# Gated linear attention with two heads below each other in the partitions: 64x64 tiles, no zero padding, output products between the outer products, and head sums ahead of the layer norm

## The reference

```python
b = jnp.cumsum(log_a, axis=2)
q_t = qc * jnp.exp(b); k_t = kc * jnp.exp(-b); k_s = kc * jnp.exp(b_last[:, :, None] - b)
att = jnp.einsum('bnihd,bnjhd->bnhij', q_t, k_t)        # inside a chunk
att = jnp.where(causal, att, 0.0)
o_intra = jnp.einsum('bnhij,bnjhe->bnihe', att, vc)
def step(state, xs):
    o_i = jnp.einsum('bihd,bhde->bihe', q_i, state)     # query times the state before the chunk
    new_state = dec[..., None] * state + jnp.einsum('bjhd,bjhe->bhde', k_i, v_i)
```

```python
v = _layernorm(jax.nn.gelu(v), ln_g, ln_b)     # first branch
q = _rmsnorm(q, q_g); k = _rmsnorm(k, k_g)     # second branch, per head
```

## Time and profile before

| | before |
|---|---|
| median of 3 runs | 1688.66 us |
| the profiled execution | 1690.31 us, its span 1688.5 us |
| PE busy | 1618.3 us (96%) |
| DVE, ACT busy | 1005.9 us (60%), 729.7 us (43%) |
| first transpose of the recurrence to the first gate matmul, layers 0 and 1 | 264.17 to 287.02 us, 783.46 to 808.02 us |
| PE waiting in group `u` and at the start of `za` | 0.55 and 1.70 us in layer 0, 0.56 and 1.74 us in layer 1 |

### The profile page before, as it was taken

One profiled execution on the slowest core, in us unless ns is written; L12 is line 12 of the kernel. 1 busy time (PEld: TensorE's weight loads), 2 busy tenths in 40 slices (PEclk: granted clock), 3 DMA queues, 4 the chain that ended last, 5 costly groups with the idle time before them and its releaser, 6 DMA issues.

```text
span 1688.5 us, 21496 instructions
## 1 busy us (share of the span) xinstructions
PE 1618.3 (96%) x8009; PEld 1326.6 (79%) x8009; DVE 1005.9 (60%) x2246; ACT 729.7 (43%) x1503; POOL 57.8 (3%) x80
## 2 busy tenths in 40 slices
PE   6999999999999999999999999999989999998999
PEld 6878777788887878777788887999767789985667
DVE  4597656444444397757443344486876554788663
ACT  4444443333234443543332434434456553354662
POOL 0000002000001000002000001000000010000000
PEclk9999999999999999999999999999999999999999
DMA  6332121323323223112233323332112233211121
GB/s 219 93 92 71 42 63 51 100 88 100 100 94 96 85 87 88 51 50 63 76 96 92 99 90 110 104 88 60 57 38 69 76 95 92 83 56 38 38 76 62
DMA packets 80883, 136.23 MB, mean 81 GB/s; under 512 B 8190, under 2 KB 33420, under 8 KB 80780
## 3 DMA queue, kind: packets, MB, share of 16 engines
q1 hardware_dynamic: 77264, 129.48, 25.7%
q10 hardware_dynamic: 3516, 5.37, 1.0%
HBM read 132.74 MB, written 2.10 MB: 80 GB/s over the span
## 4 chain that ended last, share of the span: by engine, by line
PE 46%; DVE 13%; ACT 4%; issue 2%; POOL 0%; ACTq 0%; DVEq 0%
PE gemm_bank L695 35%; PE aux_bank L762 3%; PE aux_bank L791 3%; DVE w_lo L1343 2%; PE aux_bank L779 2%; DVE rope L1442 1%; DVE head_sums L1395 1%; ACT w_hi L1021 1%; DVE probs L1498 1%; ACT probs L1068 1%; DVE kT L1482 1%; PE aux_bank L750 1%; DVE probs L1510 1%; ACT L1296 0%; PE aux_bank L939 0%
## 5 line engine op out<-in xcount | busy, mean ns | idle before, releaser
L1021 ACT ACTIVATE w_hi<-raw 128x512 fp32r<-128x512 f32 (+3 forms) x524 | 305.5, 587 | 673.3 <-PE gemm_bank L695 671.9
L1343 DVE TENSOR_TENSOR w_lo<-raw,w_hi 128x512 fp32r<-128x512 f32 (+3 forms) x524 | 329.9, 636 | 441.9 <-ACT w_hi L1021 440.2
L695 PE MATMUL gemm_bank<-act_hi,w_hi 128*128 128x512 f32 x768 | 316.7, 412 | 10.9 <-DVE mq_flat L1383 3.7
L695 PE MATMUL gemm_bank<-act_hi,w_lo 128*128 128x512 f32 x768 | 300.2, 391 | 0.0
L695 PE MATMUL gemm_bank<-act_lo,w_hi 128*128 128x512 f32 x768 | 299.9, 391 | 0.0
L695 PE MATMUL gemm_bank<-w_hi,act_hi 128*128 128x384 f32 (+3 forms) x736 | 269.3, 366 | 6.4 <-DVE bq L1383 2.9
L695 PE MATMUL gemm_bank<-w_lo,act_hi 128*128 128x384 f32 (+3 forms) x736 | 257.2, 349 | 0.0
L695 PE MATMUL gemm_bank<-w_hi,act_lo 128*128 128x384 f32 (+3 forms) x736 | 257.2, 349 | 0.0
L695 PEld LDWEIGHTS gemm_bank<-act_hi,w_hi 128*128 128x128 f32 x768 | 144.6, 188 | 47.9 <-issue 12.7
L695 PEld LDWEIGHTS gemm_bank<-act_lo,w_hi 128*128 128x128 f32 x768 | 144.8, 189 | 31.9 <-issue 2.9
L695 PEld LDWEIGHTS gemm_bank<-act_hi,w_lo 128*128 128x128 f32 x768 | 144.5, 188 | 31.0
(11 more groups left out here) (289 smaller groups left out, 2132.7 us busy)
## 6 DMA issues: line engine op xcount, KB each, us to landing
raw<-in_w_in SPq DMA_DIRECT2D x104, 512.0 KB, 3.5
raw<-in_w_in SPq DMA_DIRECT2D x64, 384.0 KB, 3.3
raw<-in_w_out SPq DMA_DIRECT2D x32, 512.0 KB, 3.7
raw<-in_w_branch SPq DMA_DIRECT2D x24, 512.0 KB, 3.7
raw<-in_w_mem_kv SPq DMA_DIRECT2D x8, 512.0 KB, 3.8
raw<-in_w_in SPq DMA_DIRECT2D x16, 256.0 KB, 2.8
raw<-in_w_in SPq DMA_DIRECT2D x8, 416.0 KB, 4.8
x<-in_x SPq DMA_DIRECT2D x4, 512.0 KB, 5.2
```

The costliest lines, as they stand in the source:

```text
L695: last = pe.matmul(o, a, c, start=begin and n == 0, stop=end and n == 2)
L1021: act.activation(w_hi[:, s % RING, 0:n], raw[:, p % RAW, kk % PIECE, 0:n], ACT.Copy)\
L1343: dve.tensor_tensor(w_lo[:, s % RING, 0:n], raw[:, p % RAW, kk % PIECE, 0:n], w_hi[:, s % RING, 0:n].bitcast(F32), ALU.subtract).then_inc( ...
```

## The change

- `kt_pad` becomes `kt_dn`, one plain product of 128x1024 on DVE, ahead of which DVE waits for `yb_lo_ready`, a semaphore that its own earlier instructions raise; L919's successor multiplies 64 rows of it for each head, the two heads of a pair in alternation into two banks.
- The outer product of a chunk is four matmuls of 64x64 tiles and 128 columns, two heads below each other in PSUM; the state is 128x128 for a pair, its copy for chunk 0 is one instruction and each later chunk takes two updates of 128x128.
- Query times state is four matmuls of 64x64 tiles and 128 columns a chunk. The outputs are kept by half (256 tokens) and by odd or even head in four banks.
- PE's order: outer products of chunks 0 and 1, att by v for the first half, then outer products in turn with query times state, then the second half, whose banks 0 and 1 are those of the outer products.
- POOL no longer zeroes kt_pad and state.
- In `prepare()` the head norm stands ahead of the layer norm of `vn`.

```diff
+            rows = [slice(hh * DK, (hh + 1) * DK) for hh in range(2)]
+            for m in range(2):
+                banks = [aux_open((1, l, "att", 2 * m + hh), 2 * m + hh) for hh in range(2)]
                 for t in range(NT):
-                    last = pe.matmul(bank[:, t * P:(t + 1) * P], kt_pad[:, h // 2, h % 2, t * P:(t + 1) * P],
-                                     qk_c[:, h // 2, t * P:(t + 1) * P], start=True, stop=True)
+                    for hh, r in enumerate(rows):
+                        last = pe.matmul(banks[hh][:, tok], kt_dn[r, m, tok], qk_c[r, m, tok], start=True, stop=True)
...
+            def outer(n):
+                bank = aux_open(key, n % 2)
                 for m in range(2):
-                    last = pe.matmul(bank[:, m * 2 * DV:(m + 1) * 2 * DV], ks_tok[half, n // 2, m * P:(m + 1) * P],
-                                     vc[half, n // 2, m * 2 * DV:(m + 1) * 2 * DV], start=True, stop=True)
+                    for hh, r in enumerate(rows):
+                        h = 2 * m + hh
+                        last = pe.matmul(bank[r, m * DV:(m + 1) * DV], ks_tok[half, n // 2, h * DK:(h + 1) * DK],
+                                         vc[half, n // 2, h * DV:(h + 1) * DV], start=True, stop=True)
...
+            for half in range(2):
+                banks = [aux_open((1, l, "o", half, hh), (2, 0)[half] + hh) for hh in range(2)]
...
+                for n in range(4 * half, 4 * half + 4):
+                    if n == 0:
+                        continue
+                    if n < 4:
+                        outer(next(chunks))
                     aux_wait_read(pe, (1, l, "U", n - 1))
                     for m in range(2):
-                        last = pe.matmul(bank[par * CHUNK:(par + 1) * CHUNK, m * 2 * DV:(m + 1) * 2 * DV],
-                                         qk_c[:, m, n * CHUNK:(n + 1) * CHUNK], state[:, n - 1, m, :],
-                                         start=False, stop=(par == 1 and m == 1), skip_group_check=True)
+                        for hh, r in enumerate(rows):
+                            last = pe.matmul(banks[hh][par, c:c + DV], qk_c[r, m, n * CHUNK:(n + 1) * CHUNK],
+                                             state[r, n - 1, m, :], start=False, stop=end, skip_group_check=True)
+                for n in chunks if half == 0 else ():
+                    outer(n)
...
                 for m in range(2):
-                    for hh in range(2):
...
-                            ins = dve.scalar_tensor_tensor(out=state[r, n, m, c], in0=state[r, n - 1, m, c],
-                                                           scalar=decay[r, m, n:n + 1], in1=new,
-                                                           op0=ALU.mult, op1=ALU.add)
+                    ins = dve.scalar_tensor_tensor(out=state[:, n, m, :], in0=state[:, n - 1, m, :],
+                                                   scalar=decay[:, m, n:n + 1], in1=bank[:, m * DV:(m + 1) * DV],
+                                                   op0=ALU.mult, op1=ALU.add)
...
+                yield
+                yield from head_norm([q[:, t, :, :] for t in range(NT)] + [k[:, t, :, :] for t in range(NT)])
                 dve.wait_ge(sg_loaded, 64 * (l + 1))
                 dve.wait_ge(rstd_ready, job + 3)
...
-                yield from head_norm([q[:, t, :, :] for t in range(NT)] + [k[:, t, :, :] for t in range(NT)])
```

More of the change, by code:

```diff
@@ L476, in read_of, with o_heads @@
         return aux_read[aux_place[key][0]]
+    def o_heads(half, hh):
+        return o_tok[:, 2 * half:2 * half + 2, :].rearrange("p t (m s e) -> p t m s e", m=2, s=2)[:, :, :, hh, :]
     def flat_2(name):
@@ L914, in gla @@
             wait_gemm_read(pe, gi_of(1, l, "vc"))
[L915 to L917 removed]
+            rows = [slice(hh * DK, (hh + 1) * DK) for hh in range(2)]
+            for m in range(2):
+                banks = [aux_open((1, l, "att", 2 * m + hh), 2 * m + hh) for hh in range(2)]
                 for t in range(NT):
[L919 to L921 removed]
+                    tok = slice(t * P, (t + 1) * P)
+                    for hh, r in enumerate(rows):
+                        last = pe.matmul(banks[hh][:, tok], kt_dn[r, m, tok], qk_c[r, m, tok], start=True, stop=True)
+                        if t == NT - 1:
+                            last.then_inc(full_of((1, l, "att", 2 * m + hh)), 1)
@@ L931, in gla @@
                 last.then_inc(full_of(key), 1)
[L932 to L935, removed]
-                    for h in range(GH):
[L937 to L942, removed]
+            chunks = iter(range(T // CHUNK - 1))
@@ new lines, in gla @@
+            for n in range(2):
+                outer(next(chunks))
+            for h in range(GH):
+                aux_wait_read(pe, (1, l, "att", h))
+            for half in range(2):
+                banks = [aux_open((1, l, "o", half, hh), (2, 0)[half] + hh) for hh in range(2)]
+                for t in range(2):
+                    for h in range(GH):
+                        c = (2 * t + h // 2) * DV
+                        pe.matmul(banks[h % 2][:, c:c + DV], att[:, h, 2 * half + t, :],
+                                  vc[:, 2 * half + t, h * DV:(h + 1) * DV],
+                                  start=(t == 0 and h < 2), stop=False, skip_group_check=True)
+                for n in range(4 * half, 4 * half + 4):
@@ L950, in gla @@
-                last.then_inc(full_of(key), 1)
+                        c = (n // 2 % 2 * 2 + m) * DV
+                        for hh, r in enumerate(rows):
+                            end = n % 4 == 3 and m == 1
+                            last = pe.matmul(banks[hh][par, c:c + DV], qk_c[r, m, n * CHUNK:(n + 1) * CHUNK],
+                                             state[r, n - 1, m, :], start=False, stop=end, skip_group_check=True)
+                            if end:
+                                last.then_inc(full_of((1, l, "o", half, hh)), 1)
@@ L1178, in block_1 @@
             evict(g_zc, ACT.Silu, lambda b: zc[:, b, :])
[L1179 to L1182, removed]
+            for i, (half, hh) in enumerate(((0, 0), (0, 1), (1, 0), (1, 1))):
+                split.beside(gi_of(1, l, ("gate", 0, 0)), i + 1)
+                bank = aux_wait_full(act, (1, l, "o", half, hh))
+                n = NT * l + i
                 if n >= 2:
                     act.wait_ge(o_sq_read, n - 1)
-                act.activation(o_tok[:, t, :], bank[:, :], ACT.Copy)
-                act.activation(o_sq[:, t % 2, :], bank[:, :], ACT.Square).then_inc(read_of((1, l, "o", t)), 1)
+                act.activation(o_heads(half, hh), bank[:, :].rearrange("p (t m e) -> p t m e", t=2, m=2), ACT.Copy)
+                act.activation(o_sq[:, i % 2, :], bank[:, :], ACT.Square)\
+                   .then_inc(read_of((1, l, "o", half, hh)), 1)
             def merge(j, i):
```

52 lines of the change are left out of this document (20 added, 32 removed).

## The result

The changed kernel took 1673.55 us (median of four runs, 1672.92 to 1674.69) against 1688.71 for the kernel before (1687.91 to 1690.15) on the same chip: ratio 0.991, 95% interval [0.9893, 0.9927]. The profiled execution took 1672.92 us with a span of 1671.1, against 1690.31 and 1688.5. The forecast was 1674.8 with a range of 1669 to 1683.

What follows compares the result with a forecast made beforehand. PE, busy 96% of the span, was taken as the bound, with DVE's chain in the recurrences' first 13 us. Recurrences 11.7 us plus heads 2.2 gave 13.9 us gained, hence 1674.8 us; range 1669 to 1683.

Steps and rivals of the forecast that it cites:

- (a): Recurrence start, transposes and products inside chunks: DVE's first copy of att starts 2.4 us in.
- (b): Recurrence, DVE's four copies of att: the last one ends 4.9 us in.
- The 3.0 us: First att copy's start if 128-column weight loads of different row tiles can't run together; sum 0.6 us a layer worse.
- (c): Recurrence, first half of att by v, then chunk 2's outer product: in PSUM at 7.6 us, DVE waiting some 1.5.
- (d): Recurrence, chunks 2 to 6: 0.95 us each, 4.8 together, states done about 12.4 us in.
- (e): Recurrence, second half's att by v and queries by state: 4.0 us together, gate group at 16.4 at full clock.
- rival 2: Recurrence with four tiles at once and no low clock: 15.5 us a layer, 1670.0 us in all; chance 0.13.
- The clock: Recurrences: one stretch of 3.41 us at half clock in each layer, counted as 1.5 us, making 17.9 a layer.
- Rivals 1, 3 and 4: Small tiles not overlapping, 1681.6 us, 0.14; each tile change draining the array, 1706, 0.03; doubled DVE update cost, 1683.2, 0.05.
- The heads: Head sums ahead of the layer norm: DVE done at 138.1 us, gain 1.1 us a layer, 2.2 in all.
- The bound of 0: Lower bound of the head sums' gain, if DVE idles 2.8 us; the upper bound was 5.6.
- the sign that the prediction gave: Forecast called wrong if the first turn of the attention in layer 0 comes later than 139.3 us.

Runs made afterwards that it cites:

- halves: Changed kernel with each state update split by head into two of 64x128, four a chunk: 1685.35 us, ratio 0.9975 to the kernel before.
- half_fill: Kernel before, plus idle matmuls of 512 and 256 columns behind each outer product of chunks 3 to 6: 1686.31 us, ratio 0.9985.
- outer_first: Changed kernel with all seven outer products ahead of all outputs, without interleaving: 1674.85 us, ratio 0.9916 to the kernel before.
- columns: Changed kernel with each state update split into two of 128x64, four a chunk: 1679.43 us, ratio 0.9946 to the kernel before.
- heads_only: Kernel before with only the head norm moved ahead of the layer norm: 1690.36 us, ratio 1.0006.
- heads_fill: Changed kernel with the layer norm's first step laid into DVE's waits for ACT's squares, two yields fewer: 1668.78 us, ratio 0.9881 to the kernel before.
- zeroed: Changed kernel with GpSimd zeroing the state area again ahead of the att products: 1675.7 us, one run.

## Why the prediction was right, and where two terms were wrong

The time was in the range and 1.3 us from the forecast, but that closeness is luck. It is the difference of two errors: the recurrence gained 17.5 us instead of 11.7, the heads 0 instead of 2.2. And the sum of 13.9 us stood against 17.4 in the profiled spans, 3.5 us off; the forecast came close because the medians differ by 15.2 us only.

- **(a), (b):** the first copy of att started 2.2 us in (2.4 predicted), the last ended at about 4.8 (4.9). Row tiles overlap although each loads 128 columns. The 3.0 us that the prediction drew from the load's duration, in case such loads can't run together, did not come, since 32 records, the change of shape included, took 2.20 us, 0.137 us a pair. The Trainium skill ("TensorE: Matmul & The Clock Gate", "Packing small matmuls") lets each further tile start some 4 ns after the one before; the trace agrees in kind, as a pair takes 0.025 us more than one record of the whole array (0.112), where two behind each other would take 0.224. In layer 1 PE waited 0.44 us for the key copy, 0.3 at most predicted.
- **(c):** 7.8 us instead of 7.6, DVE's wait 1.97 instead of 1.5.
- **(d):** five chunks took 3.9 us (272.02 to 275.94), 4.8 predicted. The price of 0.40 us an update was taken from updates that alternate between partitions. `halves` against the changed kernel shows it. States done at 11.7 instead of 12.4.
- **(e):** 3.1 us instead of 4.0. The step that failed is the reading of the earlier trace rows as two tiles per slot and no more: of rows and columns four tiles ran together, 0.034 us a record instead of 0.055 (1.09 us instead of 1.75); rival 2's 0.9 was nearer. Att by v and its restart took 2.0 instead of 2.2.
- **The clock:** predicted was one stretch at half clock in each layer, 1.5 us. There was none. `half_fill` prices a stretch at 1.67 us and the lack of any in the two recurrences, against three before, at 4.3 to 4.9. `outer_first`, `halves` and `columns`, which lengthen PE's waits or gather its work in one block, each brought half clock back, and `half_fill`, which fills PE's waits, removed it from the kernel before.

For layer 0 these make 17.9 - 0.7 - 0.9 - 1.5 = 14.8 us; 14.87 was measured. That is rival 2 in mechanism. Rivals 1, 3 and 4 fell by the same rows: no drain between tiles of one shape, no double price for 128 partitions.

- **The heads:** the waits of `u` and `za` went and DVE became late, as predicted, but 1.1 us later than said: 139.2 instead of 138.1. The idle time was 1.83 us instead of 1.6. About 0.6 us more is one `w_lo` that now stands ahead of the heads' last piece (two `w_lo` are left behind it at 139.27, three in the earlier trace rows), since the pieces moved across a step's border. The rest, some 0.3 us, was not traced. The bound of 0 was the right end, and the turn at 139.34 us is the sign that the prediction gave for this part being wrong (later than 139.3). `heads_only` shows the step failing by itself, and `heads_fill` that 2.2 us in layer 0 and 2.5 more in layer 1 were there once DVE idles less and the `w_lo` is back behind the last piece.

What stays open: when exactly half clock comes. The kernel before has the same order in both layers and shows one such stretch in the recurrence of layer 0 and two in that of layer 1. `zeroed` has one in layer 0 and none in layer 1. And the mean granted clock of the executions of the kernel before, all of them the same program, runs from 0.991 to 0.996, so that the number of stretches is not the same in each. What the clock is worth in the medians may thus differ from the 4.3 to 4.9 us of the profiles.

## What to carry to other kernels

Where PE and a second engine take turns, spread PE's independent work over its waits; one stretch at half clock cost 1.7 us here, more than any single wait of PE in that recurrence. Before moving work ahead on an engine that is busy 97% of the stretch, see what that engine will wait for in the new place, and lay other work into that wait. And take the price of an instruction from a row with the same neighbours: which partitions the one ahead of it uses can be over a quarter of it (0.38 against 0.27 us from start to start here).

## What the runs showed of the hardware that was not expected

- Four tiles of 64x64 at once: 32 float32 records of 128 columns in 1.09 us, 0.034 a record, against 0.112 for records over the whole array. Two row tiles with 128-column loads: 0.069.
- DVE in float32 with one operand in PSUM: four updates of 64x128 in 1.48 us when the partitions alternate, four of 128x64 in 0.86, two of 128x128 in 0.61. One of 64x128 lasts as long as one of 128x128 (0.35 and 0.34 us), but the next starts after 0.38 us in the one case and after 0.27 in the other.
- Two idle matmuls behind each of four outer products, where PE had waited about 0.5 us for DVE (`half_fill`), took away 3.4 us at 1.2 GHz in layer 0 and 6.8 us in layer 1.
